# Weight sums begun later and split in three pieces, three subtractions moved in the first FFN, and one attention head back in the usual order

## The chip, the cores and the metric

The kernel runs on one core of a Trainium2 chip. The metric is the device time of one execution in microseconds (us), lower is better: 2132.39 us for the kernel before, the median of 3 runs (2131.72 to 2132.82). A core has a matrix engine (TensorE, PE in the profile), a vector engine (VectorE, DVE), a scalar engine (ScalarE, ACT), a general one (GpSimd, POOL), and queues of DMA transfers that SyncE (SP), ACT and POOL issue and that 16 DMA engines carry out together. Each engine works through its own instructions in the order in which they are written; between engines only semaphores order anything.

## What is computed

Two transformer blocks of 1024 features over one sequence of 512 positions, in float32:

```python
def first_block(x, ...):
    u = rmsnorm(h, norm1_g)
    (g_qkv, g_z, g_a, g_b, d_q, d_k, d_v, i_q, i_k, i_w, gate_a, gate_b) = split(u @ w_in)
    gq, gk, gv = split(silu(causal_dwconv(g_qkv, gdn_conv_w)))
    # gated delta rule: per block T = inverse of (A + I), A strictly lower triangular
    T = lax.linalg.triangular_solve(A + eye, eye, left_side=True, lower=True)
    u, w = T @ (v * beta), T @ (k * beta * exp(G))     # then a recurrence over the blocks
    o_dsa = sparse attention over the top 128 keys of an indexer
    h = h + (sigmoid(gate_a) * o_gdn + sigmoid(gate_b) * o_dsa) @ w_out
    f_gate, f_val = split(causal_dwconv(rmsnorm(h) @ ffn_w_up, ffn_conv_w) + ffn_conv_b)
    h = h + (silu(f_gate) * f_val) @ ffn_w_down        # the first FFN, "c"
    return rmsnorm(h, final_g)

def second_block(x, ...):
    h = x + fox_attention(rmsnorm(x))     # 16 heads of 64, softmax with a decay bias
    h = h + swiglu(rmsnorm(h))            # "s"
    h = h + mla_attention(rmsnorm(h))     # 16 heads
    h = h + swiglu(rmsnorm(h))            # "m"
    return rmsnorm(h)
```

## The kernel before

**Panels.** Weights come as panels of 128 output features by 1024 inputs, 512 KB each, and PE takes them one after the other for the whole kernel. A product of float32 is made of three faster ones: high part by high part, low by high and high by low. So each panel passes through SP's load into one of two alternating buffers (`b_raw`), ACT's copy of its high part (`b_wh`, `split_hi`, L344), the low part as a difference on DVE or sometimes on POOL (`b_wl`, `split_lo`, L355), and 24 matmuls of some 0.227 us, 5.45 us in all (L552, L553, L555). A buffer is free again when the low part has been made, so a load runs about two panels ahead. A semaphore `mm_done` counts the panels whose products are done.

**The start.** Panel 0 and panels 1 to 24 make key, query and value of the delta rule, 25 to 40 its gate. The order of all that is written out by hand in steps per panel. `conv_load` is SP's list: behind panels 16 and 18 it writes the matrices A to memory (L1303), at 19 it reads their 32x32 diagonal blocks back in another layout (the semaphore `d_u` counts them), at 29 it writes the solved blocks of the inverse (L1314, waits for DVE's `solve` by `g_w`), and ahead of panels 30 and 31 it reads the inverse as PE needs it (`read_t`, L1327, waits for the writes by `d_w`). PE turns what was read (L1820) and ACT and PE go on from there (L1631, L1891, L1839). POOL's `gdn_pool` (from L1776) waits for the same writes.

**Weight sums.** From the FFNs on part of the weight panels are used in a scheme with seven products in place of eight, for which sums of quarters of the weights are needed. They are made in memory by DMAs alone, 1 MB each: `copy_quarter` (L930) copies a quarter into `scr_sums`, `add_sum` (L938) adds another quarter or another sum onto it, and there are 56 of each. Copy i+1 is issued behind add i; add i waits on a semaphore until all copies up to its own and all adds before it have landed. The first 13 (`EARLY`) are issued by POOL at the program's start, seven of them (`FIRST_EARLY`) before it waits for the triangle blocks, six behind. The later copies are ACT's, and the later adds POOL's. Nothing needs a sum before the first FFN.

**The first FFN.** Its hidden features come in three groups of panels (`ch` 0 to 2). For each tile q DVE computes the convolution's taps (L766), a product silu(gate) times value (`product`, L798) and, since the down projection also is of seven products, three subtractions on the hidden tile (`down_sum`, L1074, L1076, L1077). In `ch` 1 the product goes to one shared tile `pr`, so the three subtractions of tile 6 stand ahead of product 7, which overwrites it.

**FoX heads.** Attention runs a head per step: while PE computes head h, ACT makes the exponentials of head h+1 (`exps`, L2624) and the high part of the turned probabilities of head h (`turned`, L2630), DVE the low part (`low`, L2698), the scaling (`scaled`, L2715) and the query of head h+2 (`project_dve`, L2598), POOL a panel's low part (L355) and the key of head h+2 (`project_pool`, L2604 to L2608). Step 13 has an order of its own on all three engines.

Of the kernel before, what the change touches and what calls it, by code (L numbers as in the profile page):

```python
# [19 lines left out]
F32 = mybir.dt.float32  # L20
# [3 lines left out]
ACT = mybir.ActivationFunctionType  # L24
# [52 lines left out]
EARLY, FIRST_EARLY = 13, 7  # L77
# [87 lines left out]
def build(nc, I, out):  # L165
    with ExitStack() as ctx:
# [574 lines left out]

        def product_of(l, ch, q):
            return DOWN_TILES[l].product(q) if ch == 0 else pr
# [26 lines left out]
        def hidden_dve(dve, l, ch, norm=None, then=None, beside={}):  # L770
# [3 lines left out]
            def post(n, t, q, r, bank):  # L774
# [25 lines left out]
                def value():  # L800
                    if ch == 1 and q == 7:
                        for part in range(3):
                            down_sum(dve, l, 6, part)
                    taps()
                    product()
                    if n + 3 in DOWN_OF and n + 1 == BASE[f"c{ch}dn"]:
                        split_lo(dve, n + 3, 0, (n + 3) % 2, KT_OF[n + 3])
# [22 lines left out]
            if l == "c" and ch == 1:  # L830
                down_sum(dve, l, 7, 0)
                down_sum(dve, l, 7, 1)
                down_sum(dve, l, 7, 2).then_inc(sums_lo, 1)
# [30 lines left out]
        def hidden_act(act, l, ch, cnt=None, beside={}):  # L864
            first, cnt = PAIRS[ch][0], cnt or PAIRS[ch][1]

            def product_hi(q):
                act.wait_ge(prod_done, q + (HIDDEN_BEFORE[l] + first + 1))
                if ch == 0:
                    kept_hi(act, l, q)  # L870
                else:
                    act.activation(tile_of(yh, q), pr, ACT.Copy).then_inc(yh_done, 1)
# [197 lines left out]
        def down_sum(dve, l, q, part):  # L1070
            dve.drain()
            x0, x1 = product_of(l, 0, q)[:, T0], product_of(l, 0, q)[:, T1]
            if part == 0:
                return dve.tensor_tensor(x1, x1, pr[:, T1], ALU.subtract)  # L1074
            if part == 1:
                return dve.tensor_tensor(x0, x0, x1, ALU.subtract)  # L1076
            return dve.tensor_tensor(DOWN_TILES[l].third[:, q, :], pr[:, T0], x0, ALU.subtract)  # L1077
# [123 lines left out]
        def hidden_pool(pool, l, ch, beside={}):  # L1201
            first, cnt = PAIRS[ch]

            def body(q):
                if q in beside:
                    beside[q]()
                pool.wait_ge(yh_done, q + (YH[l] + first + 1))
                pool.tensor_tensor(tile_of(yl, q), pr, tile_of(yh, q).bitcast(F32), ALU.subtract).then_inc(y_ready, 1)  # L1208
            loop(pool, cnt, body)
# [858 lines left out]
        def index_pool(pool):  # L2068
# [5 lines left out]
            pool.tensor_tensor(rowT[:, :], rowT[:, :], mhalf[:, 0:NB], ALU.pow).then_inc(n_pw, 1)  # L2074
            pool.wait_ge(w_lo, IDX + 7)
# [535 lines left out]
        def heads_act(act, A):  # L2611
            for h_ in range(-1, 17):
# [43 lines left out]
                first_turned = fox and h_ == 13  # L2656
                if h_ + 1 < 16 and not first_turned:
                    exps(0)
                    if early:
                        exps(1)  # L2660
# [4 lines left out]
                if first_turned:  # L2665
                    exps(0)
# [23 lines left out]
        def heads_dve(dve, A):  # L2690
            for h_ in range(-1, 17):
# [38 lines left out]
                if A.name == "fox" and h_ < 13:  # L2730
                    project_dve(dve, h_ + 2)
# [4 lines left out]
                if A.name == "fox" and h_ == 13:  # L2736
                    project_dve(dve, h_ + 2)
# [32 lines left out]
        def heads_pool(pool, A):  # L2770
# [7 lines left out]
            for h_ in range(-1, 17):  # L2778
# [19 lines left out]
                if A.name == "fox" and h_ == 13:  # L2798
                    project_pool(pool, h_ + 2)
# [8 lines left out]
                if A.name == "fox" and 0 <= h_ < 13:  # L2808
                    project_pool(pool, h_ + 2)
# [153 lines left out]
        def _(pool):  # L2963
# [8 lines left out]
            key_copies(pool)  # L2972
            copy_quarter(pool, 0, s_sums)
            for i in range(EARLY):
# [3 lines left out]
                if i < EARLY - 1:  # L2978
                    copy_quarter(pool, i + 1, s_sums)
# [722 lines left out]
```

## Time and profile before

| | before |
|---|---|
| median of 3 runs | 2132.39 us (2131.72 to 2132.82) |
| the profiled execution | 2130.38 us, span of its instructions 2128.6 us |
| granted TensorE clock | 0.999 |
| PE busy | 2111.4 us (99%) |
| DVE busy | 1493.5 us (70%) |
| ACT busy | 1100.1 us (52%) |
| POOL busy | 561.1 us (26%) |
| DMA moved | 372.03 MB, 175 GB/s mean |

The span is the time from the first to the last instruction of one profiled execution; the execution is 1.78 us longer than it. The median belongs to other executions, without the profiler. The share of the chain that ended last is 92% PE, 3% DVE, 2% ACT, 1% DMA. In the views below a row of the timeline is: start, duration, engine, line, operation, tiles (out<-in), shapes, and in square brackets how long the engine had been idle ahead of it and what released it. DMA rows on an engine are the issue of a transfer and not the transfer. A program line often is a helper's, so one line can stand for many places.

### The profile page before, as it was taken

What the parts mean: (1) busy time and instruction counts of PE and PEld (TensorE: products, weight loads), DVE (VectorE), ACT (ScalarE), POOL (GpSimd) and SP (SyncE); (2) the same over time, 40 slices, a digit from 0 to 9 for tenths busy, and PEclk for the clock granted to TensorE, in tenths of its full rate; (3) what the DMA queues carried; (4) which work ended last, traced back from release to release, by engine and by line L of the source; (5) the groups of instructions that cost most, each with busy time, mean ns of one, the idle gap of its engine ahead of it and who ended that gap; (6) DMA issues with size and microseconds to landing.
All of it is one profiled execution on the core that took longest, in us unless ns stands there. A gap on an engine that the chain in (4) does not pass through costs nothing.

```text
span 2128.6 us, 32434 instructions
## 1 busy us (share of the span) xinstructions
PE 2111.4 (99%) x12116; PEld 1829.9 (86%) x12116; DVE 1493.5 (70%) x2423; ACT 1100.1 (52%) x1925; POOL 561.1 (26%) x474
## 2 busy tenths in 40 slices
PE   9999999999999999999999999999999999999998
PEld 6777898888888889888887899999887778999897
DVE  7768434687567687776777587878666885868775
ACT  6877443436444344353776354554445763545543
POOL 2100431143323110152674232201222222311011
PEclk9999999999999999999999999999999999999999
DMA  8987312455676575645845458987662335555673
GB/s 264 255 244 196 100 52 69 137 180 188 230 216 180 143 192 178 158 118 150 280 175 169 138 174 240 283 251 217 178 164 84 80 89 154 172 182 186 205 194 127
DMA packets 148349, 372.03 MB, mean 175 GB/s; under 512 B 39008, under 2 KB 43360, under 8 KB 132832
## 3 DMA queue, kind: packets, MB, share of 16 engines
q1 hardware_dynamic: 129600, 241.49, 34.5%
q0 software_dynamic: 10448, 76.55, 17.1%
q10 hardware_dynamic: 8144, 51.91, 7.0%
q8 instruction: 97, 1.59, 0.3%
q14 instruction: 60, 0.49, 0.1%
HBM read 356.78 MB, written 132.64 MB: 230 GB/s over the span
## 4 chain that ended last, share of the span: by engine, by line
PE 92%; DVE 3%; ACT 2%; DMA 1%; issue 1%; DVEq 1%; POOL 0%; SPq 0%; POOLq 0%; ACTq 0%
PE bank L430 8%; PE bank L431 8%; PE bank L434 8%; PE bank L552 7%; PE bank L553 7%; PE bank L555 7%; PE bank L1000 5%; PE bank L1004 5%; PE bank L1002 5%; PE bank L447 4%; PE bank L449 4%; PE bank L448 4%; PE bank L2535 2%; PE bank L1796 1%; PE bank L2563 1%
## 5 line engine op out<-in xcount | busy, mean ns | idle before, releaser
L344 ACT ACTIVATE b_wh<-b_raw 128x1024 fp32r<-128x1024 f32 (+1 forms) x312 | 321.7, 1034 | 547.3 <-PE bank L434 252.6
L355 DVE TENSOR_TENSOR b_wl<-b_raw,b_wh 128x1024 fp32r<-128x1024 f32 (+2 forms) x269 | 341.5, 1271 | 117.3 <-ACT b_wh L344 114.2
L552 PE MATMUL bank<-b_xh,b_wh 128*128 128x512 f32 x712 | 294.7, 414 | 0.5 <-DVE b_wl L355 0.4
L553 PE MATMUL bank<-b_xl,b_wh 128*128 128x512 f32 x712 | 278.1, 391 | 0.0
L555 PE MATMUL bank<-b_xh,b_wl 128*128 128x512 f32 x704 | 275.9, 392 | 0.0
L1208 POOL TENSOR_TENSOR b_yl<-b_arena,b_yh 128x512 fp32r<-128x512 f32 x42 | 64.4, 1533 | 542.3 <-ACT b_yh L1119 344.4
L430 PE MATMUL bank<-b_xh,b_wh 128*128 128x512 f32 x504 | 196.9, 391 | 0.0
L431 PE MATMUL bank<-b_xl,b_wh 128*128 128x512 f32 x504 | 196.1, 389 | 0.0
L434 PE MATMUL bank<-b_xh,b_wl 128*128 128x512 f32 x496 | 193.1, 389 | 0.0
L355 POOL TENSOR_TENSOR b_wl<-b_raw,b_wh 128x1024 fp32r<-128x1024 f32 (+1 forms) x45 | 103.9, 2309 | 228.3 <-ACT b_wh L344 190.4
L555 PEld LDWEIGHTS bank<-b_xh,b_wl 128*128 128x128 f32 x704 | 132.1, 188 | 29.2
L552 PEld LDWEIGHTS bank<-b_xh,b_wh 128*128 128x128 f32 x712 | 134.2, 189 | 23.9 <-DVE b_wl L355 0.9
L553 PEld LDWEIGHTS bank<-b_xl,b_wh 128*128 128x128 f32 x712 | 134.4, 189 | 21.2 <-issue 0.2
L1000 PE MATMUL bank<-b_seven_hi,b_more_wh 128*128 128x256 f32 x512 | 145.0, 283 | 0.0
L1004 PE MATMUL bank<-b_seven_hi,b_more_wl 128*128 128x256 f32 x512 | 144.9, 283 | 0.0
L1002 PE MATMUL bank<-b_seven_lo,b_more_wh 128*128 128x256 f32 x512 | 144.9, 283 | 0.0
L1000 PE MATMUL bank<-b_seven_hi,b_wh 128*128 128x256 f32 x496 | 140.6, 283 | 0.4 <-DVE b_wl L355 0.4
L1002 PE MATMUL bank<-b_seven_lo,b_wh 128*128 128x256 f32 x496 | 140.4, 283 | 0.0
L1004 PE MATMUL bank<-b_seven_hi,b_wl 128*128 128x256 f32 x496 | 140.4, 283 | 0.0
L355 DVE TENSOR_TENSOR b_more_wl<-b_more_raw,b_more_wh 128x1024 fp32r<-128x1024 f32 x92 | 120.0, 1305 | 27.8 <-ACT b_more_wh L344 25.5
L344 ACT ACTIVATE b_more_wh<-b_more_raw 128x1024 fp32r<-128x1024 f32 x92 | 96.4, 1053 | 39.7 <-PE bank L449 19.8
L431 PEld LDWEIGHTS bank<-b_xl,b_wh 128*128 128x128 f32 x504 | 94.7, 188 | 19.4
(585 smaller groups left out, 5566.8 us busy)
## 6 DMA issues: line engine op xcount, KB each, us to landing
scr_sums<-in_quarters POOLq DMA_DIRECT2D x37, 1024.0 KB, 8.8
scr_sums<-in_quarters ACTq DMA_DIRECT2D x35, 1024.0 KB, 5.3
b_raw<-scr_sums SPq DMA_DIRECT2D x110, 256.0 KB, 3.5
b_more_raw<-scr_sums SPq DMA_DIRECT2D x108, 256.0 KB, 3.4
scr_sums<-scr_sums POOLq DMA_DIRECT2D x24, 1024.0 KB, 8.2
b_raw<-in_quarters SPq DMA_DIRECT2D x92, 256.0 KB, 3.1
b_more_raw<-in_quarters SPq DMA_DIRECT2D x76, 256.0 KB, 3.1
scr_sums<-in_quarters ACTq DMA_DIRECT2D x8, 1536.0 KB, 8.8
```

The costliest lines, as they stand in the source:

```text
L344: act.activation(panel_hi_lo(n)[0][:, cols], raw_of(n)[:, cols], ACT.Copy).then_inc(w_hi, 1)
L355: dve.tensor_tensor(lo, raw_of(n)[:, cols], hi.bitcast(F32), ALU.subtract).then_inc(w_lo, 1)
L430: pe.matmul(bank[:, :], ph[:, w], hi[:, x, :], start=(k == 0), stop=False)
L431: last = pe.matmul(bank[:, :], ph[:, w], lo[:, x, :], start=False, stop=(n in SIDE_BY_SIDE and k == kt - 1))
L434: last = pe.matmul(bank[:, :], pl[:, w], hi[:, x, :], start=False, stop=(k == kt - 1))
L447: pe.matmul(bank, hi, ph, start=start, stop=False, skip_group_check=more)
L552: pe.matmul(bank[:, :], ph[:, w], hi[:, x, :], start=(k == 0), stop=False)
L553: last = pe.matmul(bank[:, :], ph[:, w], lo[:, x, :], start=False, stop=(n in SIDE_BY_SIDE and k == kt - 1))
L555: last = pe.matmul(bank[:, :], pl[:, w], hi[:, x, :], start=False, stop=(k == kt - 1))
L1000: pe.matmul(bank, ph[:, w], xs_hi[i][:, k, :], start=(i < 4 and k == 0), stop=False, skip_group_check=(i > 3))
L1002: pe.matmul(bank, ph[:, w], xs_lo[i][:, k, :], start=False, stop=False, skip_group_check=(i > 3))
L1004: m = pe.matmul(bank, pl[:, w], xs_hi[i][:, k, :], start=False, stop=(k == 3), skip_group_check=(i > 3))
```

## The change

Nothing is added or taken away: all engines have as many instructions as before, and the places of a few of them are others.

**Weight sums.** POOL waits until nine panels' products are done before copy 0. Ahead of the wait for the triangle blocks there are 3 adds (`FIRST_EARLY`), behind it 8, up to 11 in all (`LATE_EARLY`). Adds 11 and 12 with their copies are issued in `index_pool`, behind the last operation on the index key, each copy waiting for all sums before it.

**First FFN.** Product 7 of `ch` 1 goes to a tile of its own, `c_last`, and its readers on ACT, POOL and DVE read it there. The three subtractions of tile 6 stand behind the two splits at the end of the up projection, just ahead of those of tile 7.

**FoX head 13.** ACT's first exponentials stand ahead of the first two turned tiles again, DVE's query ahead of its first two low parts, and POOL's key behind the panel's low part, as for the heads before.

```diff
-EARLY, FIRST_EARLY = 13, 7
+EARLY, FIRST_EARLY, LATE_EARLY = 13, 3, 11
...
+        c_last = take(34 * T, T)
+
         def product_of(l, ch, q):
+            if (l, ch, q) == ("c", 1, 7):
+                return c_last
             return DOWN_TILES[l].product(q) if ch == 0 else pr
...
                 def value():
-                    if ch == 1 and q == 7:
-                        for part in range(3):
-                            down_sum(dve, l, 6, part)
                     taps()
                     product()
...
             if l == "c" and ch == 1:
+                for part in range(3):
+                    down_sum(dve, l, 6, part)
                 down_sum(dve, l, 7, 0)
...
             pool.tensor_tensor(rowT[:, :], rowT[:, :], mhalf[:, 0:NB], ALU.pow).then_inc(n_pw, 1)
+            for i in range(LATE_EARLY, EARLY):
+                pool.wait_ge(s_sums, 32 * i)
+                copy_quarter(pool, i, s_sums)
+                add_sum(pool, i)
...
-                first_turned = fox and h_ == 13
-                if h_ + 1 < 16 and not first_turned:
+                if h_ + 1 < 16:
                     exps(0)
...
                     turned(1)
-                if first_turned:
-                    exps(0)
...
-                if A.name == "fox" and h_ < 13:
+                if A.name == "fox" and h_ + 2 < 16:
                     project_dve(dve, h_ + 2)
...
                     low(1)
-                if A.name == "fox" and h_ == 13:
-                    project_dve(dve, h_ + 2)
...
-                if A.name == "fox" and h_ == 13:
-                    project_pool(pool, h_ + 2)
...
-                if A.name == "fox" and 0 <= h_ < 13:
+                if A.name == "fox" and 0 <= h_ and h_ + 2 < 16:
                     project_pool(pool, h_ + 2)
...
             key_copies(pool)
+            pool.wait_ge(mm_done, 9)
             copy_quarter(pool, 0, s_sums)
-            for i in range(EARLY):
+            for i in range(LATE_EARLY):
                 if i == FIRST_EARLY:
                     pool.wait_ge(d_u, 16 * NB)
                 add_sum(pool, i)
-                if i < EARLY - 1:
+                if i < LATE_EARLY - 1:
                     copy_quarter(pool, i + 1, s_sums)
```

The readers of the product (ACT's copy, POOL's L1208 and `down_sum`) have `product_of(l, ch, q)` in place of `pr`. Lines of the changed kernel are 4 to 8 higher than those of the kernel before, so L930 and L938 are L934 and L942 there.

On POOL, around the wait for the triangle blocks (the semaphore `gdn_dma_blocks`) and at the end of the sums ahead of the delta rule, before:

```order
L938 DMA scr_sums<-scr_sums 128x2048 [waits weight_sums_moved]
L930 DMA scr_sums<-in_quarters 128x2048
L938 DMA scr_sums<-scr_sums 128x2048 [waits weight_sums_moved,gdn_dma_blocks]
...
L938 DMA scr_sums<-in_quarters 128x2048 [waits weight_sums_moved]
L1776 TENSOR_TENSOR b_arena<-b_gdn_a,b_mats 128x512 [waits gdn_dma_inverse,gdn_inverted,masks_loaded]
```

The same engine of the changed kernel, from the last row ahead of the sums on:

```order
L1452 COPY b_rrow<-b_arena 64x512
L934 DMA scr_sums<-in_quarters 128x2048 [waits products_done]
...
L942 DMA scr_sums<-scr_sums 128x2048 [waits weight_sums_moved,gdn_dma_blocks]
...
L942 DMA scr_sums<-scr_sums 128x2048 [waits weight_sums_moved]
L1780 TENSOR_TENSOR b_arena<-b_gdn_a,b_mats 128x512 [waits gdn_dma_inverse,gdn_inverted,masks_loaded]
```

The first copy has a wait that it did not have, the wait for the blocks stands at the fourth add and not at the eighth, and the last add ahead of L1780 is number 10, which adds a sum to a sum, and not number 12.

On DVE, where the first FFN's down projection of `ch` 1 begins (L355 makes a panel's low part), before:

```order
L355 TENSOR_TENSOR b_spare_panels<-b_arena,b_spare_panels 128x1024 [waits panel_hi]
L1074 TENSOR_TENSOR b_arena<-b_arena 128x256
L1076 TENSOR_TENSOR b_arena<-b_arena 128x256
L1077 TENSOR_TENSOR b_arena<-b_arena 128x256
L766 SCALAR_TENSOR_TENSOR b_arena<-b_arena,b_vec 128x511 [waits gdn_oT]
L766 SCALAR_TENSOR_TENSOR b_arena<-b_arena,b_vec 128x510
L798 TENSOR_TENSOR b_arena<-b_arena 128x512 [waits y_tiles,gate_silu]
L355 TENSOR_TENSOR b_wl<-b_raw,b_wh 128x1024 [waits panel_hi] x2
L1074 TENSOR_TENSOR b_arena<-b_arena 128x256
```

The same place in the changed kernel:

```order
L355 TENSOR_TENSOR b_spare_panels<-b_arena,b_spare_panels 128x1024 [waits panel_hi]
L771 SCALAR_TENSOR_TENSOR b_arena<-b_arena,b_vec 128x511 [waits gdn_oT]
L771 SCALAR_TENSOR_TENSOR b_arena<-b_arena,b_vec 128x510
L803 TENSOR_TENSOR b_arena<-b_arena 128x512 [waits y_tiles,gate_silu]
L355 TENSOR_TENSOR b_wl<-b_raw,b_wh 128x1024 [waits panel_hi] x2
L1078 TENSOR_TENSOR b_arena<-b_arena 128x256
L1080 TENSOR_TENSOR b_arena<-b_arena 128x256
```

The three subtractions (L1074, L1076, L1077, which are L1078, L1080, L1081) have gone from ahead of the taps to behind the two low parts.

On POOL in step 13 of the FoX heads, before:

```order
L2786 TENSOR_TENSOR b_yl<-b_arena,b_yh 128x512 [waits y_hi,att_normalised]
L2604 TENSOR_TENSOR b_fox_kb_90<-b_ssq,b_fox_ka 64x512 [waits fox_qk_hi]
L2606 COPY b_fox_ka<-b_fox_ka 64x512
L2608 COPY b_fox_qb<-b_fox_qa 64x512
L355 TENSOR_TENSOR b_wl<-b_raw,b_wh 128x1024 [waits panel_hi,panel_lo]
```

In the changed kernel:

```order
L2789 TENSOR_TENSOR b_yl<-b_arena,b_yh 128x512 [waits y_hi,att_normalised]
L355 TENSOR_TENSOR b_wl<-b_raw,b_wh 128x1024 [waits panel_hi,panel_lo]
L2612 TENSOR_TENSOR b_fox_kb_90<-b_ssq,b_fox_ka 64x512 [waits fox_qk_hi]
L2614 COPY b_fox_ka<-b_fox_ka 64x512
L2616 COPY b_fox_qb<-b_fox_qa 64x512
```

The panel's low part stands ahead of the key of head 15 and its two copies.

## Rows read from the trace of the kernel before

**Rows 1.** PE's waits over the whole span: engine, line, waited for: us, times, longest.

```profile
PE bank L2553 <- DVE b_fox_pT L2698: 1.3, 1, 1.3
...
PE bank L552 <- DVE b_wl L355: 0.4, 1, 0.4
...
PE bank L1839 <- ACT b_gdn_y L1891: 0.2, 1, 0.2
```

**Rows 2.** Timeline of POOL, 60 to 230 us, sums 7, 11 and 12.

```profile
135.31 0.81 POOL L938 DMA_DIRECT2D scr_sums<-scr_sums  x1 [23.08 <-DMA b_gdn_y<-scr_a]
...
182.97 0.81 POOL L938 DMA_DIRECT2D scr_sums<-scr_sums  x1 [10.85 <-DMA scr_sums<-in_quarters]
...
193.42 0.81 POOL L938 DMA_DIRECT2D scr_sums<-in_quarters  x1 [9.10 <-DMA scr_sums<-in_quarters]
```

**Rows 3.** Chain of waits in order of time, 200 to 232 us: start, us, what.

```profile
215.71 2.76 DMA scr_t<-b_gdn_y
218.49 0.34 SPq L1327
...
219.34 6.79 DMA b_raw<-in_zga
...
229.66 2.00 PE bank L1839 x16
```

**Rows 4.** DMA queues, 214 to 228 us: packets, MB, share of 16 engines.

```profile
q1 hardware_dynamic: 5165, 3.14, 83.3%
```

**Rows 5.** DMA queues and landing times, 194 to 202 us.

```profile
q0 software_dynamic: 144, 1.05, 65.1%
...
b_raw<-in_zga SPq DMA_DIRECT2D x1, 512.0 KB, 3.3
```

**Rows 6.** DMA queues and landing times, 138 to 142 us.

```profile
q0 software_dynamic: 96, 0.79, 96.7%
...
b_raw<-in_gv SPq DMA_DIRECT2D x1, 512.0 KB, 8.4
```

**Rows 7.** Timeline of POOL, 360 to 406 us.

```profile
403.45 2.40 POOL L355 TENSOR_TENSOR b_wl<-b_raw,b_wh 128x1024 fp32r<-128x1024 f32 x1 [31.28 <-ACT b_wh L344]
```

**Rows 8.** Landing of L1303's writes, at 97 to 99 and 125 to 127 us.

```profile
DMA to landing us min/median/max: 10.4/10.4/10.4
...
DMA to landing us min/median/max: 2.8/2.8/2.9
```

**Rows 9.** Timeline of DVE, 796.9 to 808 us.

```profile
796.98 0.43 DVE L1074 TENSOR_TENSOR b_arena<-b_arena 128x256 f32<-128x256 f32 x1
...
798.33 1.57 DVE L766 SCALAR_TENSOR_TENSOR b_arena<-b_arena,b_vec 128x511 f32<-128x511 f32 x2
...
805.53 2.36 DVE L355 TENSOR_TENSOR b_spare_panels<-b_arena,b_spare_panels 128x1024 fp32r<-128x1024 f32 x2
```

**Rows 10.** Timeline of PE, 801 to 809 us.

```profile
801.92 0.39 PE L447 MATMUL bank<-b_yh,b_wh 128*128 128x256 f32 x1 [1.14 <-DVE b_wl L355]
...
807.77 0.28 PE L447 MATMUL bank<-b_yh,b_spare_panels 128*128 128x256 f32 x1
```

**Rows 11.** Timeline of POOL, 1142 to 1155 us.

```profile
1144.44 1.30 POOL L2604 TENSOR_TENSOR b_fox_kb<-b_ssq,b_fox_ka 64x512 fp32r<-64x512 f32 x1 [2.34 <-ACT b_fox_ka L2594]
...
1147.74 2.38 POOL L355 TENSOR_TENSOR b_wl<-b_raw,b_wh 128x1024 fp32r<-128x1024 f32 x1 [0.22 <-issue]
```

**Rows 12.** L2715 on DVE at 1148 to 1150 and 1139 to 1142 us.

```profile
L2715 DVE TENSOR_SCALAR b_arena<-b_arena x1: 1718/1718/1718, 1148.7 to 1148.7; 128x512 f32<-128x512 f32 x1
...
L2715 DVE TENSOR_SCALAR b_arena<-b_arena x4: 270/390/487, 1139.1 to 1140.4; 128x512 f32<-128x512 f32 x1, 128x384 f32<-128x384 f32 x1, 128x128 f32<-128x128 f32 x1, 128x256 f32<-128x256 f32 x1
```

**Rows 13.** Timeline of PE, 1144 to 1156 us.

```profile
1148.92 0.45 PE L2532 MATMUL bank<-b_fox_ka,b_fox_qa 128*128 128x512 f32 x1
```

**Rows 14.** Timeline of DVE, 1132 to 1142 us.

```profile
1135.33 1.15 DVE L2598 TENSOR_TENSOR b_fox_qa<-b_ssq,b_fox_qa 64x512 fp32r<-64x512 f32 x1
1137.65 1.29 DVE L2698 TENSOR_TENSOR b_fox_pT<-bank,b_fox_pT 128x512 fp32r<-128x512 f32 x2 [1.17 <-ACT b_fox_pT L2630]
```

More of the change, by code:

```diff
@@ L871, in product_hi @@
                 else:
-                    act.activation(tile_of(yh, q), pr, ACT.Copy).then_inc(yh_done, 1)
+                    act.activation(tile_of(yh, q), product_of(l, ch, q), ACT.Copy).then_inc(yh_done, 1)
             def post(n, t, q, r, bank):
@@ L1073, in down_sum @@
             if part == 0:
-                return dve.tensor_tensor(x1, x1, pr[:, T1], ALU.subtract)
+                return dve.tensor_tensor(x1, x1, product_of(l, 1, q)[:, T1], ALU.subtract)
             if part == 1:
                 return dve.tensor_tensor(x0, x0, x1, ALU.subtract)
-            return dve.tensor_tensor(DOWN_TILES[l].third[:, q, :], pr[:, T0], x0, ALU.subtract)
+            return dve.tensor_tensor(DOWN_TILES[l].third[:, q, :], product_of(l, 1, q)[:, T0], x0, ALU.subtract)
         def add_down(dve, l, i):
@@ L1207, in body @@
                 pool.wait_ge(yh_done, q + (YH[l] + first + 1))
-                pool.tensor_tensor(tile_of(yl, q), pr, tile_of(yh, q).bitcast(F32), ALU.subtract).then_inc(y_ready, 1)
+                pool.tensor_tensor(tile_of(yl, q), product_of(l, ch, q), tile_of(yh, q).bitcast(F32), ALU.subtract).then_inc(y_ready, 1)
             loop(pool, cnt, body)
```

## Prediction

> **What bounds the kernel now.** I read the page first: TensorE (PE) is busy 99% of the span at a granted clock of 0.999 (the page's rows stand in the table of the profile section), so the kernel is one long row of matmuls, and a change that takes no matmul away can only win or lose PE's idle time. Then the waits of PE, sorted by their total: the largest is 1.3 us and a single wait, all of them together are a few microseconds, and the two that matter for what follows are 0.4 us (L552, on a weight's low part) and 0.2 us (L1839, on ScalarE) [rows 1]. So there is little to win anywhere, while every delay that reaches PE is paid in full. Next the timeline of GpSimd (POOL), which issues the weight sums [rows 2]; the chain of waits between 200 and 232 us, where PE's next panel hangs on four DMAs in a row [rows 3]; and the shares and landing times of the DMAs, to see what a sum does to a load beside it [rows 4 to 8]. Last the timelines at the other two places [rows 9 to 14].
>
> The change has three parts that don't touch each other: the sums (A), three subtractions of the first FFN (B), one FoX head (C).
>
> **A, the sums.** The copies and adds stay the same 26 DMAs. Before, add 7 is released by the triangle blocks at 135.31 us and add 12 goes out at 193.42 [rows 2]. Five rounds of one copy and one add are 58.1 us, 11.6 each; the last, 182.97 to 193.42, is 10.45.
> - The start. Copy 0 now waits for nine panels, and three adds instead of seven stand ahead of the blocks. Three rounds of 11.6 us are 35 us, and from a start anywhere before about 95 us they are done by 135.31. The gap of 35 us and more ahead of the blocks frees the DMA engines there. What could PE win by it? In this stretch its waits on a weight are the 0.4 us of L552 [rows 1]; bounds 0 and 1 us. I take 0, since PE hardly waits.
> - Behind the blocks stand eight adds instead of six, 3 to 10. By their number modulo four, 3 to 8 are the same kinds of DMA as 7 to 12 were, so they take the same places and add 8 goes out at 193.42. Add 9 follows one round later and add 10 two: 193.42 + 2 x 10.45 = 214.3 at the earliest, 193.42 + 2 x 11.6 = 216.6 by the mean. Copy 10 lies just ahead of it.
> - What stands there. At 215.71 goes the last of the four writes of the inverse to memory (L1314), 2.76 us; behind it at 218.49 the reads L1327, then panel 31, whose 6.79 us end at 226.13; from there ScalarE and PE's L1839 at 229.66 [rows 3]. PE waits 0.2 us there already [rows 1], so it has no slack. SP's queue alone fills the engines to 83.3% between 214 and 228 us, 3.14 MB [rows 4].
> - The price. A lone add holds 65.1% of 8 us, 5.2 us of all 16 engines [rows 5]. Beside POOL's transfer SP's gets little: between 138 and 142 us POOL's queue has 96.7%, and a panel of 512 KB takes 8.4 us from issue to landing [rows 6], where the panel in rows 5 takes 3.3. So panel 31 lands later by about what add 10 needs, 5.2 us. The engines stand free in the 16.7% that SP leaves of these 14 us, 2.3 us, mostly in the gaps between write and read, and part of the add falls into them. Bounds: 0 if add 10's packets are through before 215, 7 us if copy 10's end holds the writes as well. I take 4.5 us, nearer the lone add's row, because panel 31 is the last in its queue and has to wait for all that went ahead.
> - Adds 11 and 12 go behind the index key. There POOL is idle 31.28 us, up to its split at 403.45 [rows 7]; two rounds of 11.6 fit. Their four DMAs lie beside panel loads in a stretch where PE waits for none. Bounds 0 and 1, taken as 0.
>
> What the Trainium skill says of such sharing, in "DMA: Bandwidth & Descriptors", section "Queues, rings and completion order": each DMA engine goes round the queues that have work, a packet from one and then a packet from the next. By that rule the writes of the inverse would get a turn behind every packet of the sum and be held little, which speaks against the dearest case below; this case's trace has 96.7% for the one queue [rows 6] and a write that lands 10.4 us after its issue instead of 2.8 [rows 8], so I leave that case its chance.
>
> **B, the FFN's subtractions.** VectorE (DVE) does three subtractions from 796.98, of 0.43 us, until taps and product 7 start at 798.33: 1.35 us ahead of the split on which PE's L447 waits 1.14 us at 801.92 [rows 9, 10]. Now they stand behind both splits, so the split ends 1.35 us earlier and the wait goes: -1.1 (its excess over the usual step between two matmuls is 1.3). What is late next: six subtractions instead of three now lie between these splits and the two of the spare panels, which begin at 805.53 as before, since the sum of DVE's work is unchanged. The first of these ends at about 806.7 (2.36 us for the two); PE, which starts on that panel at 807.77 before [rows 10], comes 1.3 us earlier, at 806.5, so 0.2 to 0.4 comes back. Gain 0.9 us; bounds 0.3 and 1.3. The new tile for product 7 takes a wait away and adds no instruction.
>
> **C, FoX head 13.** POOL computes the key of head 15 from 1144.44, and then splits a panel from 1147.74 for 2.38 us [rows 11]. Beside that split DVE's L2715 takes 1.718 us, where its four of the head before take 0.487 at most [rows 12]. It delays the heads behind it, and PE's longest wait of all, 1.3 us at L2553, comes in the next one [rows 1]. Now POOL splits first. It is idle for 2.34 us ahead of the key, so it can begin at 1142.1 and, where ScalarE's high part comes a little later, by 1142.7, and ends by 1145.1. L2715 then stands clear of it: 1.2 us less on DVE. ScalarE's exps and turns only change places, with the same sum, and so do DVE's projection and its two low parts. Price: the key and its two copies take 1144.44 to 1147.51, and begin now by 1145.2; they end near 1148.3, and PE needs them at 1148.92 [rows 13]: 0.6 us of cover. In head 12 the projection on DVE costs 1.15 instead of 0.70 us beside POOL's, but DVE then waits 1.17 us for ScalarE anyway [rows 14], which hides it. Gain 1.2 us; bounds 0 (the key is late, or PE's wait moves to ScalarE) and 2.0 (both waits go whole).
>
> The Trainium skill, "SBUF - State Buffer", section "Who interferes with whom", has an exclusive lock on the ports that VectorE and GpSimd share, for the whole of the instruction that holds it. L2715 ends at 1150.40, 0.28 us behind the end of POOL's split at 1150.12, so the trace agrees that it was blocked and not slowed. By the rule alone the gain would be the whole 1.23 us.
>
> **The sum.** The profiled execution took 2130.38 us (span 2128.6 and 1.8 around it). +4.5 - 0.9 - 1.2 = +2.4 gives 2132.8. The median of the runs, 2132.39, is 2.0 above the profiled one, so the forecast on its scale is 2134.8, which is +0.11%.
>
> **Rivals.**
> 1. The sum is hidden, only B and C are left: 2132.39 - 2.1 = 2130.3. It holds if the two rounds are short because the engines are quiet behind 203 us, so that add 10's packets end before the writes, or if they fit into SP's gaps. For it: the 16.7% left [rows 4]. Against it: even rounds of 10.45 put its issue at 214.3, and its packets then need 5.2 us more [rows 5].
> 2. The dear one, slower: copy 10's tail and add 10 hold the write of the inverse, which is made of short packets, then its reads and panel 31 behind both. The write goes from 2.8 to 10.4 us as at 97.5 us [rows 8], which is +7.6; with -2.1 that gives +5.5, 2137.9. It decides if copy 10 is still on the engines at 215, that is if add 10 goes out later than about 217. Against it: the mean puts it at 216.6.
> 3. The relief in the first 130 us is worth something that PE's waits don't show, 1 to 2 us more, with A's price half as large: about 2128.5.
> 4. C does nothing or costs (the key late by a few tenths): within 1.2 us of the forecast, 2136.0.
>
> **How the numbers follow.** Forecast with its own range 2132.5 to 2136.6: 0.46. Rival 1: 0.24. Rival 2: 0.16. Rival 3: 0.07. Rival 4: 0.07. 0.2% is 4.3 us, about what a measurement of this kernel can tell from no change: faster than 2128.1 is little but the lower half of rival 3 and an unnamed rest, 0.08; slower than 2136.7 is most of rival 2 with the upper edge of the forecast and of rival 4, 0.21; the rest, 0.71, is within. The range from 2129.6 to 2138.4 takes in rivals 1 and 2 at their own values and leaves out 2 in 10.
>
> **What would show it.** On POOL: add 8 at about 193.4, add 10 between 214 and 217. If it goes out before 212, A costs nothing. The reads L1327 landing in 10 us and more instead of 6.5, panel 31 at 230 to 231, a wait of PE at L1839 or at the transposes ahead of it of 4 to 5 us. If the four writes themselves take more than 5 us, rival 2. At 802 no wait of L447, a new one of 0.3 near 806.5. In head 13 L2715 at 0.49, POOL's key by 1148.5, PE's dots on time; L2553's wait smaller. The forecast is wrong if PE's idle time between 200 and 235 us stays under 1 us, or if a new wait of over 1 us appears anywhere else.

## The result and the profile after

| | before | changed |
|---|---|---|
| median of 22 runs each | 2131.61 us | 2135.64 us |
| lowest and highest | 2129.82, 2133.45 | 2131.14, 2139.66 |
| profiled execution, span | 2130.38, 2128.6 | 2139.66, 2137.8 |
| granted clock | 0.999 | 0.997 |

The ratio is 1.0019, 95% interval 1.0013 to 1.0025: 4.0 us slower, against a forecast of 2134.8 us (+2.4). The profiled execution of the changed kernel is the slowest of its 22, so its trace shows the price of the sums at its dearest and not at its median; that must be kept in mind with every number below.

The waits of PE in the changed kernel (engine, line, waited for: us, times, longest), which answer to [rows 1]; lines are 4 to 8 higher than before, L1824 turns the inverse that was read:

```profile
PE bank L1824 <- DMA b_arena<-scr_t: 8.7, 1, 8.7
PE bank L2561 <- DVE b_fox_pT L2703: 1.2, 2, 0.7
...
PE bank L552 <- DVE b_wl L355: 0.4, 1, 0.4
...
PE bank L447 <- DVE b_spare_panels L355: 0.3, 1, 0.3
```

One wait of 8.7 us is new. L447's 1.1 us have become 0.3. The 1.2 us of L2561 are two pieces: 0.4 us are left of the 1.3 us at L2553 before, and 0.7 us stand in head 13, where PE did not wait before.

POOL's sums (timeline: start, us, engine, line), answering to [rows 2]:

```profile
63.61 0.75 POOL L934 DMA_DIRECT2D scr_sums<-in_quarters  x1 [32.09 <-PE bank L555]
...
96.59 0.81 POOL L942 DMA_DIRECT2D scr_sums<-scr_sums  x1 [11.44 <-DMA scr_sums<-in_quarters]
...
136.87 0.81 POOL L942 DMA_DIRECT2D scr_sums<-scr_sums  x1 [38.94 <-DMA b_gdn_y<-scr_a]
...
198.82 0.80 POOL L942 DMA_DIRECT2D scr_sums<-in_quarters  x1 [10.93 <-DMA scr_sums<-in_quarters]
...
212.03 0.81 POOL L942 DMA_DIRECT2D scr_sums<-in_quarters  x1 [11.88 <-DMA scr_sums<-in_quarters]
212.57 0.81 POOL L934 DMA_DIRECT2D scr_sums<-in_quarters  x1
223.01 0.81 POOL L942 DMA_DIRECT2D scr_sums<-scr_sums  x1 [9.63 <-DMA scr_sums<-in_quarters]
```

The start and the order are as forecast, the times behind the blocks are not. The six rounds from 136.87 to 212.03 take 12.5 us on average and not 11.6. So add 8, forecast for 193.4, goes out at 198.82, add 9 goes out at 212, copy 10 right behind it, and add 10, forecast for 214 to 217, only at 223. The chain of waits there, answering to [rows 3] (start, us, what):

```profile
215.80 0.33 SPq L1318
...
216.83 5.72 SPq L1318
...
222.59 3.50 DMA scr_t<-b_gdn_y
...
226.10 7.71 DMA b_arena<-scr_t
...
233.94 1.94 PE bank L1824 x8
235.89 0.43 PE bank L552
```

The third write of the inverse (L1318) holds SP's queue for 5.72 us. The reads start at 226.10 instead of 218.49, and the first takes 7.71 us. The four writes (engine, tiles, count: issue in ns min/median/max, and their landing) before, where no issue took over 0.623 us, and in the changed kernel:

```profile
L1314 SPq DMA_DIRECT2D scr_t<-b_gdn_y x4: 325/590/623, 214.1 to 215.7; - x4
...
DMA to landing us min/median/max: 2.1/2.6/2.8
```

```profile
L1318 SPq DMA_DIRECT2D scr_t<-b_gdn_y x4: 326/590/5717, 215.8 to 222.6; - x4
...
DMA to landing us min/median/max: 3.5/7.9/8.2
```

The queues in the middle of them (packets, MB, share of 16 engines), answering to [rows 4, 6]:

```profile
q0 software_dynamic: 255, 1.96, 88.9%
q1 hardware_dynamic: 107, 0.01, 1.1%
...
scr_t<-b_gdn_y SPq DMA_DIRECT2D x3, 128.0 KB, 8.1
```

The writes land in 7.9 us in the middle (median) where they took 2.6 before. Between 214 and 222 us, while three of them wait, POOL's queue has 88.9% of the engines and SP's 1.1%. Add 10 goes out only at 223.01, so what holds the writes in this execution is copy 10, issued at 212.57, with the end of add 9; add 10 lies on the reads and the panel behind them. Then PE's clock (stretch: us, busy us of PE, PEld, DVE, ACT, POOL, PEclk, DMA share, GB/s):

```profile
225.00:233.00 8.00, 0.21 (x1) 0.00 (x0) 1.15 (x1) 1.63 (x2) 6.67 (x6) 0.68 0.97 236
233.00:236.00 3.00, 2.06 (x9) 2.09 (x10) 1.71 (x2) 0.67 (x2) 2.92 (x3) 0.50 1.05 388
236.00:238.00 2.00, 2.00 (x6) 1.52 (x6) 0.50 (x1) 1.98 (x3) 0.74 (x1) 0.50 0.70 281
238.00:240.00 2.00, 2.00 (x19) 1.94 (x18) 0.73 (x1) 1.89 (x3) 0.65 (x1) 0.96 0.24 37
```

PEclk falls to 0.50 during the wait, and it is there until about 238 us: PE works at 1.2 GHz instead of 2.4, and a matmul of a panel starts every 0.43 us (235.89 in the chain is such a step) where it was 0.23. PE's sequence of instructions is the same in all these kernels, so two traces can be laid on each other instruction by instruction. Against the trace of the kernel with the other two parts alone (`e7_ffn_fox` below) the changed kernel is 0.4 us late at 15 us, 9.3 at the first transpose of the inverse, 11.35 at 238.2 us, and 11.0 at the first L1843, whose own short wait is gone. So the wait costs 8.9 us, and the stretch at the lower clock 2.0 more, 1.6 net. The forecast had no term for the clock. Not all of the 1.6 need be the clock's, since the reads and the panel behind the first one are late too: in an execution whose clock stayed at 1.00 (`e6_nowait` below) the same stretch lost 0.6 net.

At the FoX head L2715 took 1.718 us [rows 12]; now it is L2720 and takes 0.489 at most:

```profile
L2720 DVE TENSOR_SCALAR b_arena<-b_arena x4: 282/382/489, 1158.8 to 1159.8; 128x512 f32<-128x512 f32 x1, 128x384 f32<-128x384 f32 x1, 128x128 f32<-128x128 f32 x1, 128x256 f32<-128x256 f32 x1
```

### The profile page after: what moved, and what is told of

Same layout as the page of the kernel before. It is cut to its first block, busy times and chain, and to the rows that moved or that the text cites. A ratio compares the mean times of both kernels' runs of the same rounds, so it can differ in the third digit from the quotient of the medians.

```text
span 2137.8 us, 32434 instructions
## 1 busy us (share of the span) xinstructions
PE 2113.2 (99%) x12116; PEld 1831.7 (86%) x12116; DVE 1489.9 (70%) x2423; ACT 1100.6 (51%) x1925; POOL 561.0 (26%) x474
## 4 chain that ended last, share of the span: by engine, by line
PE 91%; DVE 3%; ACT 2%; DMA 2%; issue 1%; DVEq 1%; SPq 0%; POOL 0%; POOLq 0%; ACTq 0%
PE bank L430 8%; PE bank L431 8%; PE bank L434 8%; PE bank L552 7%; PE bank L553 7%; PE bank L555 7%; PE bank L1004 5%; PE bank L1006 5%; PE bank L1008 5%; PE bank L447 4%; PE bank L449 4%; PE bank L448 4%; PE bank L2543 2%; PE bank L1800 1%; PE bank L2571 1%; PE bank L2570 1%
## 5 line engine op out<-in xcount | busy, mean ns | idle before, releaser
L355 DVE TENSOR_TENSOR b_wl<-b_raw,b_wh 128x1024 fp32r<-128x1024 f32 (+2 forms) x269 | 338.9, 1262 | 124.6 <-ACT b_wh L344 121.7
L355 POOL TENSOR_TENSOR b_wl<-b_raw,b_wh 128x1024 fp32r<-128x1024 f32 (+1 forms) x45 | 103.9, 2309 | 201.8 <-ACT b_wh L344 164.2
L552 PEld LDWEIGHTS bank<-b_xh,b_wh 128*128 128x128 f32 x712 | 134.5, 189 | 24.0 <-DVE b_wl L355 0.9
L553 PEld LDWEIGHTS bank<-b_xl,b_wh 128*128 128x128 f32 x712 | 134.7, 189 | 21.2 <-issue 0.2
L355 DVE TENSOR_TENSOR b_more_wl<-b_more_raw,b_more_wh 128x1024 fp32r<-128x1024 f32 x92 | 119.0, 1294 | 33.0 <-ACT b_more_wh L344 30.7
L430 PEld LDWEIGHTS bank<-b_xh,b_wh 128*128 128x128 f32 x504 | 94.6, 188 | 19.5
```

The source lines that it names most:

```text
L355: dve.tensor_tensor(lo, raw_of(n)[:, cols], hi.bitcast(F32), ALU.subtract).then_inc(w_lo, 1)
L430: pe.matmul(bank[:, :], ph[:, w], hi[:, x, :], start=(k == 0), stop=False)
L552: pe.matmul(bank[:, :], ph[:, w], hi[:, x, :], start=(k == 0), stop=False)
L553: last = pe.matmul(bank[:, :], ph[:, w], lo[:, x, :], start=False, stop=(n in SIDE_BY_SIDE and k == kt - 1))
```

## The experiments

Each is compared with the kernel before on the same chip in the same session; "+" is slower. Kernels that stand beside the same median of before shared its runs.

**The parts alone.** Sums alone (`e1_sums_alone`): the diff shown ahead, without the FFN and the head. FFN alone (`e2_ffn_alone`), head alone (`e3_fox_alone`), and these two together (`e7_ffn_fox`): the same diff, without the lines on the sums.

> The kernel before with the change of the weight sums alone (start behind nine panels, three adds ahead of the triangle blocks, eight behind, two behind the index key); the FFN and the FoX head as before. Theory: copy 10 and add 10 lie on the inverse's writes, its reads and panel 31. The whole change moved the median by +4.0 us and I put the other two parts at -2.1, so this alone is +6.1 over the kernel before, with one wait of PE of 4 to 9 us at the transposes of the inverse (L1820 of before), add 10 going out between 214 and 223. Rival (the other two parts gain nothing, or cost): +4.0 or less here. Rival (the loss is of another part of the change): within 1 us of the kernel before and no such wait.

> The kernel before with the other two parts alone: the three subtractions of the first FFN moved, and FoX head 13 in the usual order; the weight sums as before. Theory: -2.1 us (0.9 of the FFN, 1.2 of the head), bounds -0.3 and -3.3; no wait of PE at L447 of 1.1 us, L2715 in head 13 at 0.49 us. Rival (waits only move to the next releaser): 0.

> The kernel before with the three subtractions of the first FFN moved, and product 7 in a tile of its own, alone. Theory: PE's wait of 1.1 us at L447 goes and 0.2 to 0.4 come back at the spare panel: -0.9 us, bounds -0.3 and -1.3. Rival (the whole gain of the two parts, 2.1 us, is the head's): 0.

> The kernel before with FoX head 13 in the usual order, alone. Theory: L2715 at 0.49 us instead of 1.72, PE's wait of 1.3 us at L2553 goes for the most part: -1.2 us, bounds 0 and -2.0. Rival (POOL's key of head 15 comes late and PE waits for it instead): 0 or slower, with a wait at L2532.

| | median, us | before | ratio, 95% interval |
|---|---|---|---|
| sums alone | 2138.27 (6 runs) | 2131.76 | 1.0033 [1.0021, 1.0044] |
| FFN and head | 2129.70 (11) | 2131.76 | 0.9988 [0.9979, 0.9997] |
| FFN alone | 2130.00 (11) | 2131.25 | 0.9995 [0.9987, 1.0004] |
| head alone | 2129.80 (11) | 2131.25 | 0.9993 [0.9984, 1.0002] |

The sums alone cost 6.5 us, the other two parts give 2.1 back, and 6.5 - 2.1 = 4.4 is the change's 4.0 within what the runs can tell. The two small parts one by one are inside their own noise (1.3 and 1.5 us faster by the medians), and the interval of both together goes from 0.6 to 4.5 us; their place is read from the traces. PE of the FFN-and-head kernel against before, as the difference of the start of the same instruction: -1.22 us at L447, where PE waited at 801.92 [rows 10], and -0.79 behind the spare panel, where a small wait took its place (timeline of PE in that kernel):

```profile
806.87 0.39 PE L447 MATMUL bank<-b_yh,b_spare_panels 128*128 128x256 f32 x1 [0.26 <-DVE b_spare_panels L355]
```

Across head 13 the difference goes from -0.8 to -2.0, which is 1.2 us. That is the sum of a loss and a gain. At 1145.8 us PE now waits, which it did not before, and loses 0.8:

```profile
1145.81 0.44 PE L2556 MATMUL bank<-b_mats,b_arena 128*128 128x128 f32 x2 [0.72 <-DVE b_fox_pT L2698]
```

Then it gains 2.1 in three steps, at 1147.8, 1150.1 and 1152.3. The head alone (`e3_fox_alone`) shows the same loss, and the same steps of gain. The loss comes from the changed order: the first low part on DVE starts 0.8 us later than before against the work around it, since ScalarE's exponentials, which again stand ahead of the turned tiles, hold the tile that it needs. The query that now stands ahead of it on DVE, 1.14 us beside POOL's work where it took 0.70 before, ends only 0.2 us before that tile comes:

```profile
1145.07 1.29 DVE L2698 TENSOR_TENSOR b_fox_pT<-bank,b_fox_pT 128x512 fp32r<-128x512 f32 x2 [0.20 <-ACT b_fox_pT L2633]
```

Over its whole span the trace of the FFN-and-head kernel is only 0.9 us shorter than the one before (2127.7 and 2128.6): 1.1 of the 2.0 us are lost again at 1530 and 2088 us. Whether these losses belong to the change or to the one execution isn't known.

In the sums-alone kernel, where add 10 goes out at 224.69, a little behind the 214 to 223 expected, the waits are those of the changed kernel and of the kernel before:

```profile
PE bank L1820 <- DMA b_arena<-scr_t: 8.6, 1, 8.6
...
PE bank L447 <- DVE b_wl L355: 1.1, 1, 1.1
```

**How many sums stand behind the blocks, and behind the index key.**

```diff
e4:  -EARLY, FIRST_EARLY, LATE_EARLY = 13, 3, 11   +... = 13, 3, 10
e9:                                                +... = 13, 4, 11
e5:                                                +... = 13, 5, 11
e10: +... = 13, 7, 11  and  -            pool.wait_ge(mm_done, 9)
```

> The changed kernel with one sum fewer ahead of the delta rule: seven adds behind the triangle blocks (3 to 9), three (10 to 12) behind the index key. Theory: what costs is what the DMA engines still have to do for POOL from 215 us on. Add 9 goes out at 204 to 212 us and needs about 8 us, so it ends at the edge of the writes: +0 to +3 over the sums as before, with -2.1 of the other parts between -2 and +1 us against the kernel before, and 3 to 6 us faster than the changed kernel (2135.6). Rival (the start behind nine panels or the adds behind the index key are what costs): as slow as the changed kernel, +4, or slower, since three adds now stand behind the index key.

> The changed kernel with four adds ahead of the triangle blocks and seven behind (4 to 10), two behind the index key as in the change. Theory: what counts is how late the last add behind the blocks is; with seven it goes out at 204 to 212 us, so its packets end at 212 to 220, at the edge of the inverse's writes. Between the sums as before and the change: 0 to +3 us over the FFN-and-head kernel (2129.7), that is 2129.7 to 2132.7, and no wait at POOL's split behind the index key. Rival (the number of sums behind the blocks doesn't matter, the two behind the index key do): as the changed kernel, 2135.6.

> The changed kernel with five adds ahead of the triangle blocks instead of three: six behind (5 to 10), two behind the index key, the start still behind nine panels. Theory: add 10 goes out near 193 to 199 us, where add 12 stood in the kernel before, so no wait at the transposes: -2.1 us against the kernel before, 2129.5. Five rounds of 11.6 us from 63 end at 121, ahead of the blocks at 135. Rival (the late start or the index key is what costs): +4 as in the changed kernel.

> The FFN and head parts of the change, and of the sums' part only the two behind the index key: no wait at the start, seven adds ahead of the blocks as before, four behind (7 to 10), two behind the index key. Theory: the two sums behind the index key are hidden, as add 12 is issued some 6 us before POOL's next split is ready: 2129.7, within 1 us of the kernel with those two parts alone. Rival (they cost by their transfers beside panel loads, or by POOL coming late as with three of them): 1 to 4 us more, and a wait of PE on POOL's L355 between 400 and 420 us.

| | ahead, behind the blocks, behind the key | median, us | before | ratio, 95% interval |
|---|---|---|---|---|
| changed | 3, 8, 2 | 2135.64 | 2131.61 | 1.0019 [1.0013, 1.0025] |
| `e9_first4` | 4, 7, 2 | 2130.70 | 2131.24 | 0.9998 [0.9989, 1.0006] |
| `e5_first5` | 5, 6, 2 | 2131.16 | 2131.76 | 0.9998 [0.9989, 1.0006] |
| `e10_index_two` | 7, 4, 2, early start | 2129.67 | 2131.24 | 0.9994 [0.9985, 1.0002] |
| `e4_late10` | 3, 7, 3 | 2136.74 | 2131.76 | 1.0026 [1.0017, 1.0034] |

With seven or fewer behind the blocks and two behind the key, the loss against the kernel before is gone. Not all of the gain is there: `e5_first5` was expected at 2129.5, and is 1.5 us above the FFN-and-head kernel, which ran in the same session (2129.70). Its trace has no wait at the transposes, so where these 1.5 us are stays open; `e8_ten_later` below has the same late start and the same two sums behind the key, and lies at 2129.72. `e9_first4` is inside its range; its trace has a wait of 0.6 us at the transposes. `e4_late10` came out otherwise than expected: it also has seven behind the blocks, and is 5 us slower than the kernel before. Its trace shows no wait at the transposes but another one, and POOL's timeline says why:

```profile
PE bank L552 <- POOL b_wl L355: 4.0, 1, 4.0
```

```profile
373.06 0.66 POOL L933 DMA_DIRECT2D scr_sums<-in_quarters  x1
378.85 0.86 POOL L941 DMA_DIRECT2D scr_sums<-scr_sums  x1 [5.13 <-DMA scr_sums<-in_quarters]
392.21 0.55 POOL L933 DMA_DIRECT2D scr_sums<-in_quarters  x1 [12.49 <-DMA scr_sums<-scr_sums]
398.20 0.81 POOL L941 DMA_DIRECT2D scr_sums<-scr_sums  x1 [5.45 <-DMA scr_sums<-in_quarters]
408.14 0.55 POOL L933 DMA_DIRECT2D scr_sums<-in_quarters  x1 [9.13 <-DMA scr_sums<-scr_sums]
413.43 0.81 POOL L941 DMA_DIRECT2D scr_sums<-in_quarters  x1 [4.75 <-DMA scr_sums<-in_quarters]
413.99 4.94 POOL L355 TENSOR_TENSOR b_wl<-b_raw,b_wh 128x1024 fp32r<-128x1024 f32 x2
```

A copy behind the key waits for the add ahead of it to land, so the first round there is 5.8 us from copy to add and 13.4 from add to copy, 19 in all, and the second 6.0 and 9.9, 16 in all. The third copy goes out at 408, add 12 at 413.43, and POOL's split for a panel, which stood at 403.45 before [rows 7], comes at 413.99; PE waits 4.0 us, and then works at the lower clock:

```profile
416.00:419.00 3.00, 2.33 (x6) 1.86 (x7) 0.00 (x0) 0.00 (x0) 3.00 (x4) 0.50 1.06 268
419.00:422.00 3.00, 3.00 (x9) 2.38 (x8) 2.23 (x7) 0.00 (x0) 0.66 (x3) 0.55 0.98 205
```

So my expectation, and the prediction's own rounds of 11.6 us behind the key, had the wrong round: ahead of the delta rule a copy runs beside the add ahead of it, and behind the key it comes after it. With two sums this is hidden by a few microseconds only. In the changed kernel (timeline of POOL) 4.37 us of idle time are left between add 12 and the split, and not the 8 that two rounds of 11.6 would leave:

```profile
409.20 0.81 POOL L942 DMA_DIRECT2D scr_sums<-in_quarters  x1 [5.52 <-DMA scr_sums<-in_quarters]
414.39 2.39 POOL L355 TENSOR_TENSOR b_wl<-b_raw,b_wh 128x1024 fp32r<-128x1024 f32 x1 [4.37 <-ACT b_wh L344]
```

**When the last pair goes out, and which half of it costs.** Adds 3 to 9 behind the blocks as in the change, add 10 (and in e8 its copy too) at some 250 us (copy 10 at 246.22 and add 10 at 251.67 in e8, add 10 at 248.31 in e11):

```diff
-            for i in range(LATE_EARLY):
+            for i in range(LATE_EARLY - 1):
...
                     gdn_scales(pool, i + 1)
+                if i == 0:
+                    copy_quarter(pool, LATE_EARLY - 1, s_sums)     # e8 only
+                    add_sum(pool, LATE_EARLY - 1)
```

> The changed kernel, but copy 10 and add 10 are issued by POOL behind its scales of the second pair of heads (some 245 us, where it is idle for 10 us) and not ahead of the delta rule; adds 3 to 9 stay behind the blocks, start and index key as in the change. Theory: time and not number is what counts. Without add 10 on the engines at 215 to 230 us the wait at the transposes goes or falls under 2 us: 2129.7 to 2132. Rival (seven sums behind the blocks, or the late start, already cost most): over 2134.

> The changed kernel with copy 10 issued where the change has it (behind add 9) and only add 10 moved to some 245 us. It tells apart what copy 10 and what add 10 cost. Theory as predicted (add 10 is the cost, the copy alone is done before 215): near the kernel with both moved, 2130 to 2132. Rival, the dear case of the prediction (add 9 goes out at 212 and copy 10 right behind it, both held against the inverse's short writes): 2 to 4 us above it, 2132 to 2135, with the writes L1314 landing in 6 us and more instead of 2.6.

`e8_ten_later`: 2129.72 against 2131.24, ratio 0.9992 [0.9984, 1.0001]. `e11_copy_only`: 2130.55 against 2131.24, 0.9995 [0.9987, 1.0004]. Moving the one pair by some 30 us takes 5 to 6 us away; it isn't the number of sums. With copy 10 left in place the median is 0.8 us higher, which the runs don't separate from nothing. So by the medians most of the price is add 10's, as forecast, and not copy 10's hold on the writes that the dear trace above shows. The trace of `e11_copy_only` has a little of that hold (copy 10 went out at 207.04 there): writes and wait,

```profile
L1317 SPq DMA_DIRECT2D scr_t<-b_gdn_y x4: 325/582/3069, 215.3 to 219.4; - x4
...
DMA to landing us min/median/max: 3.1/4.6/5.5
```

```profile
PE bank L1825 <- DMA b_arena<-scr_t: 1.8, 1, 1.8
```

**The disputed cost by itself.** The FFN-and-head kernel, sums as before, plus two copies of 1 MB at 214 us that nothing needs:

```diff
+            pool.wait_ge(g_w, 1)
+            copy_quarter(pool, 48, s_sums)
+            copy_quarter(pool, 49, s_sums)
             gdn_pool(pool)
+            pool.wait_ge(s_sums, 32 * (EARLY + 1))
```

(and later waits on `s_sums` raised by the two).

> The kernel with the FFN and head parts alone, its sums as before, and two extra copies of 1 MB that POOL issues when the inverse is solved (about 214 us), into places of the sums that are overwritten with the right copies much later. Nothing else is moved, so this is the disputed cost by itself. Theory: what costs is POOL's traffic on the 16 DMA engines beside the inverse's writes and reads and panel 31. Two copies need about as much of the engines as one add (5 to 6 us), so 4 to 7 us over 2129.7, with a wait of PE at the transposes of over 3 us. Rival (the loss in the changed kernel comes from POOL's order of work, its wait for the sums): within 1 us of 2129.7, since POOL itself is not kept waiting here.

2137.95 us against 2131.25, ratio 1.0030 [1.0018, 1.0041]: 8.3 us over the FFN-and-head kernel's median of the other session (8.8 if each is taken against its own before), above the 4 to 7 expected. POOL waits for the copies only ahead of its work on the index, long after they have landed, so it is the traffic. PE's wait is again at the transposes, and the writes land nearly four times as late as before:

```profile
PE bank L1823 <- DMA b_arena<-scr_t: 5.8, 2, 5.5
```

```profile
DMA to landing us min/median/max: 2.1/9.6/11.2
```

**The start.** The changed kernel without `pool.wait_ge(mm_done, 9)`.

> The changed kernel without its wait for nine panels at the start: copy 0 at 31.6 us, three adds ahead of the blocks, eight behind, two behind the index key. Theory: the start is worth nothing to PE, so it is as slow as the changed kernel, 2135.6, within 1 us. Rival (the late start saves a microsecond or two that PE's waits don't show, or costs them): 1 to 2 us off.

2134.98 us against 2131.25, 1.0018 [1.0009, 1.0027], as the changed kernel: the late start is worth nothing that can be measured, either way. Its profiled execution is a mild one, and shows what goes with a low price (POOL's timeline, its writes and its wait):

```profile
193.64 0.80 POOL L941 DMA_DIRECT2D scr_sums<-in_quarters  x1 [9.09 <-DMA scr_sums<-in_quarters]
...
204.08 0.81 POOL L941 DMA_DIRECT2D scr_sums<-in_quarters  x1 [9.11 <-DMA scr_sums<-in_quarters]
...
216.66 0.81 POOL L941 DMA_DIRECT2D scr_sums<-scr_sums  x1 [11.24 <-DMA scr_sums<-in_quarters]
```

```profile
DMA to landing us min/median/max: 2.8/3.2/3.2
```

```profile
PE bank L1823 <- DMA b_arena<-scr_t: 2.5, 1, 2.5
```

Here the last rounds before it were 10.4 us, add 9 went out at 204 and add 10 at 216.66. The writes were hardly held (3.2 us), only the reads behind them (8.6 us in the middle), PE waited 2.5 us, and its clock stayed at 1.00:

```profile
224.00:227.00 3.00, 0.80 (x4) 0.33 (x2) 0.00 (x0) 0.33 (x1) 2.92 (x4) 1.00 0.94 264
227.00:230.00 3.00, 2.25 (x12) 1.67 (x13) 2.24 (x2) 3.00 (x5) 2.81 (x2) 1.00 0.97 365
230.00:233.00 3.00, 3.00 (x22) 2.74 (x22) 1.63 (x2) 2.97 (x5) 1.34 (x2) 1.00 0.59 195
```

The span is 2.8 us over that of the FFN-and-head kernel (2130.5 and 2127.7), that of the changed kernel's trace 10.1. The changed kernel can do about either: its 22 runs lie between 2131.14 and 2139.66 us, 1.4 to 10.0 over the FFN-and-head kernel's median, and 13 of them between 2134.3 and 2135.9. The runs of the kernel before have 3.6 us between them in the same session, 6.1 at most in another. No trace of an execution in the middle was kept.

## Why the prediction was right, point by point

- **The sum's place.** "Panel 31 lands later by about what add 10 needs": right in kind, that add 10 costs by its traffic. Shown by moving that one pair (-5 to -6 us) and by adding like traffic, two copies, to a kernel without it (+8.3 us). PE waited at the transposes of the inverse, a step ahead of panel 31: the reads were late first. `e11_copy_only` puts most of the price on add 10.
- **Its price**, the term that was mis-sized: 4.5 us forecast, 6.1 measured (4.0 of the change plus 2.1 of the other parts; 6.5 alone), inside the bounds 0 and 7. The one trace that keeps the forecast's timetable (add 8 at 193.64, add 10 at 216.66, `e6_nowait`) lost only 2.8 us, so for its own case the forecast was too dear. The trace of the changed kernel has the dear case (add 9 at 212, copy 10 on top of the writes), which was rival 2, priced at 7.6 us for the sums, and lost 10.1. Most runs lie between these two. That the median is near the forecast is so in part luck: a case milder than priced, and rounds longer than taken. What the forecast lacked is the clock: after a wait of 4 to 9 us PE went on at 1.2 GHz, 1.6 us net in the trace of the changed kernel. Of its 22 runs 19 have a mean clock of 0.998 or less, of the 11 of the FFN-and-head kernel none has.
- **The rounds.** Mean 11.6 us and shortest 10.45 were read from one trace. The way from the blocks to add 9 is six rounds: 68.5 us in one trace (135.58 to 204.08, `e6_nowait`) with a wait of 2.5 us, 75.2 in another (136.87 to 212.03) with one of 8.7, and 75.4 in the sums-alone kernel (138.37 to 213.79) with one of 8.6. So in these three traces the length of the rounds goes with the price. Why a given execution has the one or the other stays open; nothing here sets it.
- **The rule on turns.** The prediction read the Trainium skill ("DMA: Bandwidth & Descriptors", section "Queues, rings and completion order": each engine goes round its queues packet by packet) as speaking for the short writes. The trace of the changed kernel counts 255 packets of POOL's queue and 107 of SP's in those 8 us: SP does get turns, somewhat fewer than half as many. In `e12_injected`, between 217 and 222 us, the counts are nearly equal, 228 and 224, and the shares 96.7% and 3.7%. POOL's packets are 7.7 KB (1.96 MB by 255) and SP's some 0.1 KB, so turns by packet leave it 1.1% to 3.7% of the time. These counts agree with the rule, if a packet of the profile is what the rule means by one, which no run shows. Read so, the rule speaks for the dear case, and I had it the wrong way round.
- **Behind the index key**: hidden, as forecast, but by another sum (from copy 11 to add 12 it is 26.1 us, 383.07 to 409.20, and not two rounds of 11.6), with 4.4 us to spare, which a third sum overdrew.
- **The start and the relief ahead of the blocks** (rival 3): nothing that can be measured, as forecast. `e6_nowait` has no late start and costs the same. `e8_ten_later` has the late start and three sums ahead of the blocks, `e10_index_two` the early start and seven, and their medians are 2129.72 and 2129.67. The rival's own value had a wrong sum: 2132.39 - 2.1, with half of A's price added and 1 to 2 us taken off, is 2130.5 to 2131.5 and not 2128.5.
- **B**: 0.9 forecast, 0.8 in the traces, with the new wait of 0.26 us at 806.87, where 0.2 to 0.4 near 806.5 was expected. **C**: 1.2 forecast, 1.2 in the traces, L2720 at 0.49 us in the changed kernel; the key of head 15 ends 0.6 us ahead of PE's use of it, as forecast, so rival 4 did not hold. But the forecast let ScalarE's exponentials and turns, and DVE's query and low parts, change places at no cost, and the new wait of 0.7 us in head 13 says otherwise: 0.8 us lost that the sum had at nothing, and 2.1 gained where it had 1.2. That the two make 1.2 is luck. Together 2.1 forecast, 2.1 by the medians, where the interval is wide (0.6 to 4.5).
- **Rival 1** (the sum hidden) did not hold for the change. With one round less (`e9_first4`) it nearly does: 0.5 us under before by the medians, where B and C alone are 2.1 under, and the runs don't separate the two.

The fastest of these kernels are the FFN-and-head parts with the sums as before (2129.70), with two sums behind the key and the early start (2129.67), and with pair 10 at some 250 us (2129.72); all are under both kernels by the medians, the first by more than its interval against the kernel before, the other two not, and they are not told apart. So no run shows that the moves of the sums bring anything by themselves.

## What to carry to other kernels

Background transfers that cost nothing in most of a kernel can cost microseconds where a short transfer is due on which others depend: find the places where a write, its read and the next weight follow each other, and keep the bulk queue empty there by time and not by count. Where a chain of waits has its length from rounds that vary by 20%, put the last round a full round ahead of the place it must not touch. And price a wait of TensorE with its clock: after the waits of 4.0, 5.5 and 8.7 us here the engine came back at the lower one, and lost more than the wait itself.

## What the runs showed of the hardware

- A 128 KB write of short packets beside GpSimd's 1 MB transfers took 7.9 us from issue to landing instead of 2.6, SP's queue had 1.1% of the engines against 88.9%, and SP itself stood for 5.72 us at the issue of the third write (3.07 at most in `e11_copy_only`, 0.62 before).
- TensorE's granted clock fell to 0.50, which is 1.2 GHz, in waits of 4.0 us (`e4_late10`), 5.5 us (`e12_injected`) and 8.7 us. It was 1.00 again at 421.7, 234.1 and 238.2 us, where PE had begun to work at 416.7, 230.3 and 233.9. In and after a wait of 2.5 us (`e6_nowait`) it stayed at 1.00.
- VectorE's query (64x512) took 1.14 us beside GpSimd's split of a panel (`e7_ffn_fox`, 1143.7), and 0.70 us beside GpSimd's copies (kernel before, 1146.3).
